# High and low parts for the probabilities-times-values product of the fox and band heads

## The reference

```python
s = jnp.einsum('bqhd,bkhd->bhqk', qi, k).astype(jnp.float32) * scale
s = s + ci.transpose(0, 2, 1)[..., None] - ct[:, :, None, :]
s = jnp.where(kpos[None, :] <= qpos[:, None], s, NEG_INF)
p = jax.nn.softmax(s, -1).astype(v.dtype)
return jnp.einsum('bhqk,bkhd->bqhd', p, v)
```

## Time and profile before

| what | value |
|---|---|
| median of three runs | 1996.56 us |
| the profiled execution, its own time | 1995.61 us |
| its span in the profile | 1994.1 us |
| TensorE busy (matmul) | 1941.4 us, 97% |
| TensorE busy (weight load) | 1914.1 us, 96% |
| VectorE busy | 1326.1 us, 67% |
| ScalarE busy | 787.2 us, 39% |
| POOL busy | 143.0 us, 7% |
| granted TensorE clock, mean | 0.992 |

### The profile page before, as it was taken

How to read it: one execution, slowest core, us unless ns; L and a number is a source line. 1 busy time by engine, 2 the same in 40 slices (tenths; PEclk the granted TensorE clock), 3 DMA queues, 4 the chain that set the end, 5 groups by cost and what they waited for, 6 DMA issues and landing times.

```text
span 1994.1 us, 37624 instructions
## 1 busy us (share of the span) xinstructions
PE 1941.4 (97%) x15484; PEld 1914.1 (96%) x15484; DVE 1326.1 (67%) x2273; ACT 787.2 (39%) x1311; POOL 143.0 (7%) x260
## 2 busy tenths in 40 slices
PE   7989999999999999999998999999999999999995
PEld 6989999999999999999998999999999999999995
DVE  6986666666564445687887666767755535557777
ACT  6443333333223233544574433334432322344444
POOL 0010000000100000000001000000000000000000
PEclk9999999999999999999999999999999999999998
DMA  7533333332522222555663333333224222225563
GB/s 298 195 109 128 122 116 113 113 105 78 183 88 84 76 85 83 195 202 194 219 214 126 116 100 116 113 113 105 91 110 153 82 91 72 102 85 208 181 224 130
DMA packets 66691, 265.02 MB, mean 133 GB/s; under 512 B 10812, under 2 KB 20668, under 8 KB 50640
## 3 DMA queue, kind: packets, MB, share of 16 engines
q1 hardware_dynamic: 40112, 202.13, 29.2%
q0 software_dynamic: 16000, 46.54, 6.8%
q10 hardware_dynamic: 10432, 14.29, 2.0%
HBM read 233.37 MB, written 32.16 MB: 133 GB/s over the span
## 4 chain that ended last, share of the span: by engine, by line
PE 90%; DVE 5%; DMA 2%; ACT 1%; issue 1%; SPq 0%; ACTq 0%; DVEq 0%
PE GB L642 33%; PE GB L529 24%; PE GB L553 19%; PE AB L582 3%; PE AB L624 3%; PE GB L857 3%; DMA WR<-in_wt 2%; PE AB L593 2%; DVE WL L1311 1%; DVE WL L1446 1%; PE AB L629 0%; PE AB L609 0%; DVE XL L1692 0%; PE AB L632 0%; PE AB L804 0%
## 5 line engine op out<-in xcount | busy, mean ns | idle before, releaser
L642 PE MATMUL GB<-XH,WH 128*128 128x272 f32 x1392 | 408.1, 293 | 10.0 <-DVE WL L1446 5.9
L642 PE MATMUL GB<-XH,WL 128*128 128x272 f32 x1392 | 403.3, 290 | 0.0
L642 PE MATMUL GB<-XL,WH 128*128 128x272 f32 x1392 | 402.7, 289 | 0.0
L916 ACT CAST WH<-WR 128x2048 fp32r<-128x2048 f32 x120 | 229.0, 1908 | 426.5 <-PE GB L529 223.2
L1311 DVE TENSOR_TENSOR WL<-WR,WH 128x2048 fp32r<-128x2048 f32 x120 | 274.8, 2290 | 158.2 <-ACT WH L916 145.2
L975 ACT CAST WH<-WR 128x512 fp32r<-128x512 f32 (+1 forms) x224 | 165.1, 743 | 319.7 <-DVE WR L1432 143.9
L642 PEld LDWEIGHTS GB<-XH,WH 128*128 128x128 f32 x1392 | 264.4, 190 | 12.6 <-DVE WL L1446 6.7
L642 PEld LDWEIGHTS GB<-XH,WL 128*128 128x128 f32 x1392 | 264.3, 190 | 0.0
L642 PEld LDWEIGHTS GB<-XL,WH 128*128 128x128 f32 x1392 | 263.7, 189 | 0.0
L1446 DVE TENSOR_TENSOR WL<-WR,WH 128x512 fp32r<-128x512 f32 (+1 forms) x224 | 188.4, 842 | 19.8 <-ACT WH L975 16.5
L529 PE MATMUL GB<-XH,WH 128*128 128x272 f32 x1280 | 176.4, 290 | 0.0
(11 more groups left out here) (249 smaller groups left out, 2977.3 us busy)
## 6 DMA issues: line engine op xcount, KB each, us to landing
WR<-in_wt SPq DMA_DIRECT2D x120, 1024.0 KB, 4.8
WR<-in_wt SPq DMA_DIRECT2D x128, 512.0 KB, 4.4
XR<-out POOLq DMA_DIRECT2D x64, 136.0 KB, 2.9
out<-OY ACTq DMA_DIRECT2D x24, 272.0 KB, 2.2
out<-OY ACTq DMA_DIRECT2D x8, 544.0 KB, 5.3
out<-KT POOLq DMA_DIRECT2D x16, 272.0 KB, 3.5
out<-VT POOLq DMA_DIRECT2D x16, 272.0 KB, 3.5
o_rest<-OS POOLq DMA_DIRECT2D x16, 272.0 KB, 2.3
```

Source lines behind the costliest of these rows:

```text
L642: mm = pe.matmul(out, w[:, k, :], x[:, k, :], start=(start and k == 0 and i == 0), stop=(stop and k == chunks - 1 and i == 2))
L916: act.copy(WH[:, s, :, :], WR[:, s, :, :]).then_inc(hi, 1)
```

## The change

For fox and band heads alone:
- ScalarE makes a float32r high part PTH of the transposed probabilities, in three copies (512, 512 and 256 columns) out of banks 0, 1 and 2, between the high parts of d1 and a12 (last head: ahead of `w_hi`). Its copy of the turned values makes the high part VH in place of V.
- VectorE makes the low part PTL with three subtractions in place of the three copies, ahead of the low part of a12 (last head: ahead of `w_lo`) and not behind it; it now waits for `p_turned` and for each of ScalarE's copies. A new subtraction of 512 columns makes VL, the low part of the values; it waits for ScalarE's VH and stands ahead of c21.
- TensorE transposes the probabilities in another order, grouped by key block, so that a key block's query blocks lie side by side. The sample rows of the values are transposed into bank 0, after a wait for the first subtraction. `mix` also waits for VL, and runs twelve matmuls, three passes (VH x PTH, VL x PTH, VH x PTL) over four key blocks of 512, 384, 256 and 128 columns, all added up in bank 3. The sample tokens' matmuls are as before.
- PTL lies in the place of S, PTH in that of PT, VH in that of V and VL in that of BI. Nothing changes in the pairs but the name of an argument.

```diff
@@ -218,11 +218,15 @@
         VT = sb("VT", [P, TOK])
         ES = sb("ES", [P, TOK])
         GA = sb("GA", [P, TOK])
+        VH = sb_at("VH", [P, 4, HD], top[0], F32R)
         V = sb("V", [P, NT, HD])
+        PTL = sb_at("PTL", [P, 10 * P], top[0], F32R)
         S = sb("S", [P, SW])
+        PTH = sb_at("PTH", [P, 10 * P], top[0], F32R)
         PT = sb("PT", [P, PTW])
         KTC = sb("KTC", [P, PAST])
         VC = sb("VC", [P, 2, HD])
+        VL = sb_at("VL", [P, 4, HD], top[0], F32R)
         BI = sb("BI", [P, SEQ + PAST + DEC])
         BD = sb("BD", [P, TOK])
         assert top[0] <= arena_end, (top[0], arena_end)
@@ -369,6 +373,9 @@
         b_pe = sem("b_pe")
         c_copy = sem("c_copy")
         c_out = sem("c_out")
+        p_turned = sem("p_turned")
+        p_high = sem("p_high")
+        v_low = sem("v_low")
         x_sums = sem("x_sums")
         x_thi = sem("x_thi")
         x_tlo = sem("x_tlo")
@@ -432,6 +439,9 @@
 
             rows, h = ((UPPER, 0), (UPPER, 1), (LOWER, 1), (LOWER, 0))[i]
             return OY[:, rows, half(h)], TH[:, i, :, :], TLOW[:, rows, half(h)]
+
+        key_order = [(i, 0) for i in range(4)] + [(i, 1) for i in range(1, 4)] + [(3, 3), (2, 2), (3, 2)]
+        key_cols = [(0, 0, 4), (1, 4, 3), (2, 8, 2), (3, 7, 1)]
 
         def pt_col(j):
             return PT[:, P * j:P * (j + 1)]
@@ -588,6 +598,8 @@
                 pe.wait_ge(pr, 5 * u + 5)
                 j = 0
                 blocks = [(i, b) for i in range(4) for b in range(len(g.blocks[i]))]
+                if g in (FOX, BAND):
+                    blocks = key_order
                 for j, (i, b) in enumerate(blocks):
                     at = g.at[i] + P * b
                     mm = pe.transpose(AB[:, j // 4, P * (j % 4):P * (j % 4 + 1)], S[:, at:at + P], ident[:, :])
@@ -601,15 +613,15 @@
                     mm = pe.transpose(AB[0:DEC, 2, 320:320 + DEC], S[0:DEC, at:at + DEC], ident[0:DEC, 0:DEC])
                 return mm
 
-            def turn_v():
-
-                mm = pe.transpose(AB[0:DEC, 2, 352:352 + P], VT[:, SEQ:TOK], ident[:, :])
+            def turn_v(bank, at):
+
+                mm = pe.transpose(AB[0:DEC, bank, at:at + P], VT[:, SEQ:TOK], ident[:, :])
                 mm.then_inc(pt, 1)
                 for i in range(4):
                     mm = pe.transpose(AB[:, 3, P * i:P * (i + 1)], VT[:, P * i:P * (i + 1)], ident[:, :])
                 mm.then_inc(vt, 1)
 
-            def mix(g, u, kl, vu=None, dm=None):
+            def mix(g, u, kl, vu=None, dm=None, vu_low=None):
 
                 pe.wait_ge(pte, 3 * u + 3)
                 pe.wait_ge(ld_vc, 16 * (kl + 1))
@@ -618,12 +630,19 @@
                     pe.wait_ge(vse, vu + 1)
                 if dm is not None:
                     pe.wait_ge(ld_vm, 16 * (dm + 1))
-                j = 0
-                for i in range(4):
-                    for b, kb in enumerate(g.blocks[i]):
-                        mm = pe.matmul(AB[:, 3, P * i:P * (i + 1)], V[:, kb, :], pt_col(j),
-                                       start=(b == 0), stop=(b == len(g.blocks[i]) - 1))
-                        j += 1
+                if g in (FOX, BAND):
+                    pe.wait_ge(v_low, vu_low + 1)
+                    for p, (v, t) in enumerate(((VH, PTH), (VL, PTH), (VH, PTL))):
+                        for kb, j, n in reversed(key_cols) if p == 2 else key_cols:
+                            mm = pe.matmul(AB[:, 3, P * kb:], v[:, kb, :], t[:, P * j:P * (j + n)],
+                                           start=(p == 0 and kb == 0), stop=(p == 2 and kb == 0))
+                else:
+                    j = 0
+                    for i in range(4):
+                        for b, kb in enumerate(g.blocks[i]):
+                            mm = pe.matmul(AB[:, 3, P * i:P * (i + 1)], V[:, kb, :], pt_col(j),
+                                           start=(b == 0), stop=(b == len(g.blocks[i]) - 1))
+                            j += 1
                 mm.then_inc(pv, 1)
                 for b in range(g.cached):
                     mm = pe.matmul(AB[:, 2, 0:DEC], VC[:, b, :], PT[:, 10 * P + DEC * b:10 * P + DEC * (b + 1)],
@@ -721,15 +740,16 @@
                     scores(g, u, fl=l + 1)
 
                 def all_probs():
-                    turn_probs(g, u)
+                    turn_probs(g, u).then_inc(p_turned, 1)
 
                 def all_values():
                     pe.wait_ge(c_out, taken(b, "c12"))
-                    turn_v()
+                    pe.wait_ge(pte, 3 * u + 1)
+                    turn_v(0, 0)
 
                 two_tiles(l, a)
                 two_tiles(l, b, all_scores, all_probs, all_values)
-                mix(g, u, kl, vu)
+                mix(g, u, kl, vu, vu_low=l * 2 * GH + i)
 
             def pair(n, m, u, kl, vu, dm, last):
 
@@ -743,7 +763,7 @@
                 gemm(n, m, 3, 0)
                 turn_probs(SWA, u)
                 pe.wait_ge(zf[0], m + 2)
-                turn_v()
+                turn_v(2, 352)
                 gemm(n, m, 3, 1)
                 mix(SWA, u, kl, vu)
                 gemm(n, m, 4, 0)
@@ -928,6 +948,20 @@
                     s = S[0:r, g.at[i]:g.at[i] + w]
                     act.activation(s, s, ACT.Exp, bias=nmx[0:r, i:i + 1],
                                    accum_out=esum[0:r, i:i + 1]).then_inc(ex, 1)
+
+            def probs_hi(u, i):
+
+                for b in range(3):
+                    if b < 2:
+                        act.wait_ge(pt, 3 * u + b + 1)
+                    else:
+                        act.wait_ge(p_turned, i + 1)
+                    w = P * (4 if b < 2 else 2)
+                    act.copy(PTH[:, 512 * b:512 * b + w], AB[:, b, 0:w]).then_inc(p_high, 1)
+
+            def take_v_hi(vu):
+                act.wait_ge(vt, vu + 1)
+                act.copy(VH[:, :, :], AB[:, 3, :].rearrange("p (b d) -> p b d", b=4)).then_inc(ve, 1)
 
             def take_v(vu):
                 act.wait_ge(vt, vu + 1)
@@ -1044,13 +1078,16 @@
                     block_hi(b + 1, "s1")
                     block_hi(b + 1, "s3")
                 if last:
+                    probs_hi(u, l * 2 * GH + i)
                     act.wait_ge(b_pe, ran(b, "p3"))
                     w_hi(l * LT + C0, 0, l * (LT // 2) + C0 // 2 + 1)
                 else:
-                    for name in ("a11", "d1", "a12"):
+                    for name in ("a11", "d1"):
                         block_hi(b + 1, name)
+                    probs_hi(u, l * 2 * GH + i)
+                    block_hi(b + 1, "a12")
                     block_hi(b + 1, "d2")
-                take_v(vu)
+                take_v_hi(vu)
                 act.wait_ge(c_out, taken(b, "c21"))
                 act.activation(ES[:, :], GA[:, :], ACT.Tanh, scale=0.5).then_inc(eg, 1)
                 take_head(i, u, l)
@@ -1364,6 +1401,27 @@
                     s = S[0:r, g.at[i]:g.at[i] + w]
                     dve.tensor_scalar(s, s, rsum[0:r, i:i + 1], None, ALU.mult).then_inc(pr, 1)
 
+            def probs_lo(u, i):
+
+                dve.wait_ge(p_turned, i + 1)
+                for b in range(3):
+                    w = P * (4 if b < 2 else 2)
+                    dve.wait_ge(p_high, 3 * i + b + 1)
+                    low = dve.tensor_tensor(PTL[:, 512 * b:512 * b + w], AB[:, b, 0:w],
+                                            PTH[:, 512 * b:512 * b + w].bitcast(F32), ALU.subtract)
+                    if b < 2:
+                        low.then_inc(pte, 1)
+                dve.tensor_copy(PT[:, 10 * P:10 * P + 2 * DEC], AB[:, 2, 256:256 + 2 * DEC])
+                dve.tensor_copy(PT[0:DEC, 10 * P + 2 * DEC:PTW], AB[0:DEC, 2, 320:320 + DEC]).then_inc(pte, 1)
+
+            def values_lo(u, vu):
+
+                dve.wait_ge(pt, 3 * u + 3)
+                dve.tensor_copy(V[0:DEC, 4, :], AB[0:DEC, 0, 0:P]).then_inc(vse, 1)
+                dve.wait_ge(ve, vu + 1)
+                dve.tensor_tensor(VL[:, :, :], AB[:, 3, :].rearrange("p (b d) -> p b d", b=4), VH[:, :, :].bitcast(F32), ALU.subtract) \
+                    .then_inc(v_low, 1)
+
             def take_probs(g, u, vu=None):
                 n = sum(len(b) for b in g.blocks)
                 for b in range(2):
@@ -1558,11 +1616,12 @@
                     for name in ("s1", "s3", "a11", "d1"):
                         block_lo(b + 1, name)
                 take_product(b, "c12", VT[:, half(1)])
+                probs_lo(u, l * 2 * GH + i)
                 if last:
                     w_lo(l * LT + C0, 0)
                 else:
                     block_lo(b + 1, "a12")
-                take_probs(g, u, vu)
+                values_lo(u, vu)
                 take_product(b, "c21", GA[:, half(0)])
                 head_gate(i, l, u, b)
 
```

## The result

The changed kernel takes 1998.72 us (median of 14 runs, 1997.07 to 2004.02), the kernel before 1994.62 us in the runs beside it (median of 14, 1993.63 to 1998.17). The ratio is 1.0022, with a 95% interval of 1.0015 to 1.0030: the change makes the kernel slower by 4.1 us between the two medians and by some 4.4 us by the ratio, just past the 0.2% line that the forecast drew. The forecast had +3.1 us; its largest chance, "within 0.2%", lies on the near side of the line, and the interval spans it. The measured 1998.72 us lies within 1 us of the forecast's 1999.7 us, and part of that is luck: the forecast started from a median of three runs, 1996.56 us, which stands 1.9 us above the median of 14, and the change costs about 1 us more than forecast.

The account below looks back on a forecast made before the run. The prediction took TensorE to bound the kernel. A 0.54 us wait less 0.33 us saved gave +2.9 us over 14 heads, plus 0.2 us for the last two: 1996.56 + 3.1 = 1999.7 us, range 1994.3 to 2004.0 us.

Parts of the forecast that it names:

- within 0.2%: Outcome for the whole kernel: a change of under 0.2%, 4.0 us, not told from none; chance 0.55.
- What TensorE saves: In the mix: twelve float32r matmuls take 1.91 us for the old 2.24 us, saving 0.33 us a head.
- +0.03 us end: Low end of the net cost per head in 14 heads: 0.51 us wait less 0.48 us saving.
- The wait: Ahead of the mix: TensorE stands 0.54 us for VL, behind ScalarE's copy and VectorE's subtraction, in 14 heads.
- The two last heads: In each layer's last head: w_lo runs late, the mix starts 0.4 us late, net about +0.1 us each.
- The sum: Whole kernel: 2.9 us for 14 heads plus 0.2 us for the last two, +3.1 us, to 1999.7 us.
- What costs nothing: ScalarE's three new copies and VectorE's subtractions: hidden in free time, with 1.2 us free on VectorE before VL.
- Rival 1: At the mix: VL is not its last wait, so only the saving stays, 5.3 us faster, 1991.3 us; chance 0.07.
- Rival 2: Ahead of the mix: the clock falls in each new gap, +22 us, 2019 us; chance 0.04.
- Rival 3: On VectorE: shared banks double copy times, VL starts 0.7 us late, +14 us, 2011 us; chance 0.05.
- Rival 4: In the mix: twelve matmuls at 0.131 us or less take 1.57 us, total -2.3 us, 1994.3 us; chance 0.04.
- rival 5: In the mix: 128-column float32r matmuls run in four passes, 0.21 us each, +7.9 us, 2004.5 us; chance 0.03.

Follow-up runs that it names:

- vl_last_heads: Changed kernel with VL x PTH as last pass, all in bank 1, output-copy waits only where bank 1 was written: 1991.68 us, ratio 0.9984 to before.
- wait_alone: Kernel before with its old mix, plus one unused 512-column VectorE subtraction and TensorE's wait for it ahead of the mix: 2002.98 us, ratio 1.0035.
- vl_twice: Changed kernel with the VectorE subtraction that makes VL issued twice: ratio 1.0056 to the kernel before.
- narrow: vl_last_heads with every mix matmul cut to 128 columns, 30 matmuls for 12: 2008.82 us in one run.
- vl_last: Changed kernel with VL x PTH as last pass, all in bank 1, but the pairs' scores also waiting for the output copy: ratio 1.0002 to before.
- v_before_d2: Changed kernel with ScalarE copying the high part of the values ahead of d2's high part: ratio 0.9997 to the kernel before.

## Why the prediction was right

**What TensorE saves** was forecast at 0.33 us a head and is 2.24 - 1.92 = 0.32 us. The prices from the scores carried over as a sum, not one by one. In a pass that runs from wide to narrow the last, 128-column matmul takes 0.06 us and not 0.11, and the 512-column one behind it 0.28 us and not 0.23: 0.34 us for the two, as forecast. Only the pass that runs from narrow to wide has 0.11 and 0.23 us. The forecast had seen the 0.06 us step once, and its +0.03 us end took it for a saving; it isn't one.

**The wait** was forecast link by link and the links hold: ScalarE's copy to float32r 0.58 us, the hand-over to VectorE 0.03 us, the subtraction 0.69 us for 0.68, TensorE's matmul 0.15 us after it (forecast 0.05 and 0.10). The halves of that 0.15 us are not as forecast: the weight load is recorded 0.12 us after VectorE's end and the matmul 0.03 us after the load, so the sum came out right by errors that cancel. The first mix matmul stands 0.54 us later, as forecast. The recorded idle time, 0.38 us, is under my 0.4 to 0.5 us because the record counts from the modelled end of p4's last matmul, 307.59 + 0.29 = 307.88.

**The term that was too small** is the restart inside that wait. I let the first matmul cost what a steady one costs once its weights are in. In TensorE's timeline of the changed kernel, in windows of 0.01 us, it takes 0.31 us to the second. The same first matmul takes 0.23 us in vl_last_heads, where nothing holds it:

```profile
308.26 0.47 PE L637 MATMUL AB<-PTH,VH 128*128 128x512 f32 x1 [0.38 <-DVE VL L1422]
308.57 0.46 PE L637 MATMUL AB<-PTH,VH 128*128 128x384 f32 x2
...
308.87 0.22 PE L637 MATMUL AB<-PTH,VH 128*128 128x128 f32 x1
308.93 0.44 PE L637 MATMUL AB<-PTH,VL 128*128 128x512 f32 x1
309.21 0.46 PE L637 MATMUL AB<-PTH,VL 128*128 128x384 f32 x2
...
310.02 0.39 PE L637 MATMUL AB<-PTL,VH 128*128 128x512 f32 x1
...
310.25 0.19 PE L648 MATMUL AB<-PT,VC 128*128 128x32 f32 x1
```

```profile
307.42 0.40 PE L639 MATMUL AB<-PTH,VH 128*128 128x512 f32 x1
307.65 0.45 PE L639 MATMUL AB<-PTH,VH 128*128 128x384 f32 x2
```

wait_alone has it too, with other matmuls behind the wait: 0.06 us. Without the wait the load stands 0.13 us ahead of its matmul (307.29 and 307.42), behind it 0.03 us, so what the longer first step holds may be the rest of its own load; no run separates the two. So a head loses 0.29 us by the timeline and 0.32 us by the period, and not 0.21; some 0.02 us of that I can't place.

**The two last heads** were forecast at +0.1 us each. The step of the period into them is 52.99 us, +0.17 us: VectorE's w_lo holds V's sample rows to 519.88, and VL ends at 520.48, near the forecast's order of things (w_lo late by 1.65 us, VL behind it).

**The sum** by the measured periods is 14 x 0.31 + 2 x 0.17 = 4.7 us, where the forecast had 3.1, and the ratio says 4.4 us. The direction, the path and both terms were right; the size is 1.0 to 1.6 us short, most of it the restart, 14 x 0.08 = 1.1 us.

The two profiled spans differ by only 2.7 us, and most of what is missing can be placed. From the output copy of head 0 to that of head 7 the second layer takes 1494.68 - 1123.00 = 371.68 us for 369.69 before, +1.99 us, close to 6 x 0.31 + 0.17 = 2.03. The first layer takes 376.30 for 375.91, +0.39 us. There, in heads 1 and 2 and in no others, TensorE waits for the sum L1519 (L1461 before), which stands on VectorE behind weights that land late; those waits are 4.0 us before, 3.3 us after, 0.2 us in vl_twice and none in narrow. So they shrink when the heads ahead get much longer; between 52.50 and 53.45 us of period they scatter from 3.3 to 4.5 us without an order. From before to after they give back 0.6 us.

The clock gives back more: the stretch around head 2's wait had a granted clock of 0.83 before and has 1.00 after, at a wait of 2.31 and 2.02 us. Behind the wait the first thirteen steps between products take 3.10 us before, most of them 0.23 us, the 1.2 GHz level, and 1.74 us after. Together that is 2.0 us, enough for the 1.6 us by which the first layer falls short of the second. The waits, before and after:

```profile
222.29 0.59 PE L642 MATMUL GB<-XH,WH 128*128 128x272 f32 x1 [2.31 <-DVE GA L1461]
```

```profile
222.51 0.39 PE L661 MATMUL GB<-XH,WH 128*128 128x272 f32 x1 [2.02 <-DVE GA L1519]
```

The windows' columns are stretch, span, PE, PEld, DVE, ACT, POOL, granted clock and DMA; before, then after:

```profile
220.00:230.00 10.00, 7.71 (x50) 7.71 (x51) 7.77 (x15) 5.67 (x10) 0.55 (x1) 0.83 0.24 81
```

```profile
220.00:230.00 10.00, 7.98 (x64) 7.76 (x63) 7.85 (x16) 5.96 (x10) 0.55 (x1) 1.00 0.23 81
```

One execution of each kernel was profiled, so how much of this is the change and how much scatter stays open; it wasn't tested by a run of its own. It bears on a microsecond or two, and on the spread between runs of one kernel.

**What costs nothing** cost nothing that the head's period shows: VectorE waits 0.89 us for V's sample rows (forecast 0.5 to 0.9) and 1.18 us for VH (forecast 1.2), ScalarE is through with the three high copies by 303.08. vl_last_heads, which carries all of this added work and is faster, shows it best.

**The rivals.** Rival 1 (the mix doesn't wait for VL) falls by the 16 recorded waits and by vl_twice. Rival 2 (the clock falls in the gap) falls by vl_twice, whose gaps of 0.98 us leave the steps at full speed, the 2.4 GHz level. Rival 3 (VectorE late) falls by the 1.18 us that VectorE itself waits for VH; its own sum was too steep, since it left out the wait ahead of V's sample rows, 0.89 us, as a second cushion. Rival 4 and rival 5 (the mix cheaper or dearer than the rows) fall by 1.92 us for twelve matmuls and 0.11 us at 128 columns, thirty in a row. The Trainium skill, page TensorE: Matmul & The Clock Gate, section Back-to-back issue gap, has about 81 ns for that width; narrow measured 110 ns for thirty in a row with float32r, so for this data type the trace does not agree.

## What to carry to other kernels

A split into high and low parts adds a link to the chain of whatever it splits. Before the mix is costed, ask which part is made last and let the matmuls begin with the others: the same twelve matmuls were 0.2% slower than the old ones with the late operand waited for ahead of all, and 0.16% faster with it in the last pass. That took a second PSUM bank, so that TensorE doesn't write the bank that VectorE still reads (no run tried it in one bank), and a bank that changes hands brings its own waits: put them only where the bank was used, or they eat the gain, as 4.4 us did in vl_last.

## What the hardware showed that I had not expected

- A stream of matmuls behind a short wait pays beyond the wait: its first float32r matmul of 512 columns took 0.31 us, against 0.23 us in vl_last_heads, on top of 0.15 us between VectorE's end and its start. The length of the wait made no difference: it was 0.31 us at 0.38 us of idle time, at 0.98 us (vl_twice) and with none recorded (v_before_d2, 308.49 to 308.80).
- The step from one matmul to the next depends on its neighbours. At the end of a pass from wide to narrow 128 columns took 0.06 us and the 512 behind them 0.28 us; in the pass from narrow to wide 256 columns took 0.17 us (309.67 to 309.84), where elsewhere they take 0.12 us, and the load for their successor began only at 309.72. So single steps mislead, and whole passes don't: without a wait the three passes took 0.58, 0.64 and 0.70 us, 1.92 us together for a forecast of 1.91 us. No run shows that either order is dearer.
- The length of an idle stretch alone did not tell what clock was granted. TensorE's idle time of 2.31 us ahead of head 2 went with a granted clock of 0.83 in its stretch of 10 us before, and 2.02 us with 1.00 after. But in vl_last_heads 2.42 us ahead of head 1 went with 1.00, the 2.4 GHz level throughout, and in wait_alone 1.90 us ahead of head 2 with 0.83. The rows of vl_last_heads:

```profile
167.67 0.39 PE L664 MATMUL GB<-XH,WH 128*128 128x272 f32 x1 [2.42 <-DVE GA L1522]
```

```profile
160.00:170.00 10.00, 7.58 (x61) 7.36 (x60) 6.12 (x10) 3.13 (x5) 1.99 (x2) 1.00 0.06 24
```

Rival 2 was to be decided from the length of gap at which the grant is lost; these traces show no such length.
